# Reordering the first loads of a two-layer decoder trunk: one semaphore per input, adaLN columns in pairs, a held GpSimd queue, and the first norm's squares and root moved forward

## What is computed

```python
c_act = jax.nn.silu(c)
for l in range(DEPTH):                       # DEPTH = 2
    mod = c_act @ ada_w[l] + ada_b[l]        # 6 * 1024 columns
    shift1, scale1, gate1, shift2, scale2, gate2 = jnp.split(mod, 6)
    h = rms_norm(x, norm1_g[l]) * (1.0 + scale1) + shift1
    proj = h @ w_in[l]                       # q, k, v of two mixers, two gates
    ...                                      # sliding-window and stick-breaking attention
    x = x + gate1 * (merged @ w_out[l])
    h2 = rms_norm(x, norm2_g[l]) * (1.0 + scale2) + shift2
    x = x + gate2 * peer_ffn(h2, ...)        # top-16 of 128^2 experts, 8 heads, rows gathered
return rms_norm(x, final_g)
```

## Time and profile before

| | us |
|---|---|
| median of 3 runs | 1884.69 |
| lowest, highest | 1884.15, 1887.4 |
| the profiled execution's own time | 1883.45 |
| its span in the trace | 1881.6 |
| busy: TensorE / VectorE / ScalarE / GpSimd | 1534.5 / 1402.4 / 584.2 / 513.1 |

### The profile page before, as it was taken

How to read it: one execution, slowest core, us unless ns; L and a number is a source line. 1 busy time by engine, 2 the same in 40 slices (tenths; PEclk the granted TensorE clock), 3 DMA queues, 4 the chain that set the end, 5 groups by cost and what they waited for, 6 DMA issues and landing times.

```text
span 1881.6 us, 18314 instructions
## 1 busy us (share of the span) xinstructions
PE 1534.5 (82%) x6060; PEld 915.2 (49%) x6060; DVE 1402.4 (75%) x3392; ACT 584.2 (31%) x1322; POOL 513.1 (27%) x564
## 2 busy tenths in 40 slices
PE   1989899887787788787888999998778688777786
PEld 0978889333333333333367889963333233333332
DVE  5889899877767777765578989997777776767555
ACT  2445544322222122122244555522212212212221
POOL 0000003433333333333300000234333333333330
PEclk9999999988898989989999999999998999998989
DMA  8665778999999999999947668699999999999994
GB/s 349 227 222 187 257 247 365 418 421 422 421 421 421 421 421 421 422 421 421 421 179 239 192 214 285 265 414 421 421 422 421 421 421 421 422 421 421 422 422 194
DMA packets 104639, 675.73 MB, mean 359 GB/s; under 512 B 12000, under 2 KB 12128, under 8 KB 32352
## 3 DMA queue, kind: packets, MB, share of 16 engines
q0 software_dynamic: 80640, 587.24, 76.4%
q1 hardware_dynamic: 23904, 87.32, 13.3%
HBM read 673.46 MB, written 1.05 MB: 358 GB/s over the span
## 4 chain that ended last, share of the span: by engine, by line
DMA 45%; PE 32%; DVE 17%; ACT 2%; issue 2%; SPq 1%; DVEq 0%; ACTq 0%
DMA big<-pairs,big 22%; DMA late<-pairs,big 21%; PE yac L623 13%; PE acc L406 11%; DVE big L1079 2%; DVE big L925 2%; DVE wsp L385 2%; DVE late L1079 2%; DMA big<-ada_pairs 2%; PE pg L406 2%; PE acc L506 1%; PE yac L585 1%; SPq L432 1%; ACT big L777 1%; DMA big<-ada 1%
## 5 line engine op out<-in xcount | busy, mean ns | idle before, releaser
L623 PE MATMUL yac<-big 128*128 128x512 f32 x1184 | 565.3, 631 | 132.1 <-ACT big L777 132.1
L623 PE MATMUL yac<-late,big 128*128 128x512 f32 x864 | 433.9, 657 | 119.9 <-ACT big L777 119.9
L623 PEld LDWEIGHTS yac<-big 128*128 128x128 f32 x1184 | 232.7, 202 | 456.3 <-issue 269.1
L1265 POOL DMA_INDIRECT big<-pairs,big x296 | 284.6, 961 | 432.0 <-PE yac L623 391.4
L623 PEld LDWEIGHTS yac<-late,big 128*128 128x128 f32 x864 | 176.5, 210 | 374.3 <-issue 208.9
L1265 POOL DMA_INDIRECT late<-pairs,big x216 | 202.7, 938 | 380.7 <-PE yac L623 329.9
L406 PE MATMUL acc<-hs,wsp 128*128 128x256 f32 x2208 | 285.8, 288 | 0.0
L406 PEld LDWEIGHTS acc<-hs,wsp 128*128 128x128 f32 x2208 | 272.8, 194 | 7.3 <-issue 6.5
L1079 DVE CUSTOM_DVE_ANT_0 big<-big,acc 128x1024 f32<-128x1024 f32 x148 | 179.0, 1219 | 116.2 <-DMA big<-pairs,big 116.0
L768 ACT ACTIVATE big<-big 128x4 f32<-128x4 f32 (+1 forms) x138 | 28.3, 205 | 715.5 <-DVE big L1079 715.5
L777 ACT ACTIVATE big<-con,big 128x128 f32<-128x128 f32 x512 | 164.7, 390 | 247.4 <-DVE big L1094 247.2
(11 more groups left out here) (148 smaller groups left out, 1162.4 us busy)
## 6 DMA issues: line engine op xcount, KB each, us to landing
raw<-stream SPq DMA_DIRECT2D x140, 512.0 KB
big<-ada_pairs POOLq DMA_DIRECT2D x48, 1024.0 KB, 7.2
big<-ada SPq DMA_DIRECT2D x16, 512.0 KB, 15.3
big<-pairs,big POOLq DMA_INDIRECT x296, 21.5
late<-pairs,big POOLq DMA_INDIRECT x216, 22.3
big<-subkeys SPq DMA_DIRECT2D x2, 1024.0 KB, 13.2
x<-xT SPq DMA_DIRECT2D x1, 1024.0 KB, 7.1
outT<-big SPq DMA_DIRECT2D x1, 1024.0 KB, 3.9
```

Source lines behind the costliest of these rows:

```text
L623: mm = pe.matmul(yac[:, 2 * t + w, :], diag(n), row(n)[:, D + w * 512:D + (w + 1) * 512], start=(n % (SLOTS // TT) == 0), stop=(n % (SLOTS ...
L1265: g.indirect_dma_start(row(n), None, pairs, bass.IndirectOffsetOnAxis(ap=col(Q_IDX + n).bitcast(U32), axis=0)).then_inc(row_in[n % RING], 16)
```

## The change

- The five inputs are issued in another order and on four semaphores: `pos` and `con` on `con_in`, `cB` on `c_in`, `x` on `x_in`, `final_g` on `gain_in`. TensorE and VectorE wait for `con_in` at their start, ScalarE for `c_in`, and for `x_in` ahead of the squares; VectorE waits for `gain_in` ahead of the last norm.
- The 16 `ada` blocks are loaded and taken in pairs (k, 8 + k), each pair on a semaphore of its own. SP's order is: pos, con, cB, pairs 0 and 1, x, par, pairs 2 and 3, chunk 0, pairs 4 and 5, chunk 1, pairs 6 and 7, chunks 2 and 3, final_g, subkeys.
- GpSimd's first load of adaLN pairs in layer 0 waits until pair 7 has landed.
- ScalarE makes squares and root first, then the high parts of chunks 0 and 1, and that of chunk 2 behind `modulated`.
- VectorE no longer waits for the sine tables. It takes the reciprocal behind pair 4, the low part of chunk 0 behind pair 5, of chunk 1 behind pair 6, and of chunk 2 behind `source`. Behind pair 7 come a join and `next_mods`.

```diff
-            sp.dma_start(con[:, :], consts).then_inc(inputs_in, 16)
-            sp.dma_start(x[:, :], xT).then_inc(inputs_in, 16)
-            sp.dma_start(cact, cB).then_inc(inputs_in, 16)
-            sp.dma_start(cosT[:, :].bitcast(I32), pos).then_inc(inputs_in, 16)
-            sp.dma_start(fg[:, :], final_g).then_inc(inputs_in, 16)
+            sp.dma_start(cosT[:, :].bitcast(I32), pos).then_inc(con_in, 16)
+            sp.dma_start(con[:, :], consts).then_inc(con_in, 16)
+            sp.dma_start(cact, cB).then_inc(c_in, 16)
...
-            for a in range(N_ADA1):
-                sp.dma_start(ada_first(a), ada[a, :, :]).then_inc(first_ada_in[a // 4], 16)
-                if a % 4 == 3:
-                    sp.dma_start(raw[:, a // 4, :], stream[a // 4, :, :]).then_inc(landed[a // 4], 16)
+            def load_first(k):
+
+                for a in (k, KD + k):
+                    sp.dma_start(ada_first(a), ada[a, :, :]).then_inc(first_ada_in[k], 16)
+
+            load_first(0)
+            load_first(1)
+            sp.dma_start(x[:, :], xT).then_inc(x_in, 16)
+            sp.dma_start(par[:, :], params[0, :, :]).then_inc(params_in, 16)
+            load_first(2)
+            load_first(3)
+            load(0, 0, 0, 0)
+            load_first(4)
+            load_first(5)
+            load(1, 0, 0, 0)
+            load_first(6)
+            load_first(7)
+            load(2, 0, 0, 0)
+            load(3, 0, 0, 0)
+            sp.dma_start(fg[:, :], final_g).then_inc(gain_in, 16)
...
-            pe.wait_ge(inputs_in, 80)
+            pe.wait_ge(con_in, 32)
...
-            act.wait_ge(inputs_in, 80)
+            act.wait_ge(c_in, 16)
...
                 if L == 0:
-                    for m in range(AHEAD):
-                        act_high(act, L, m)
+                    act.wait_ge(x_in, 16)
                     squares(0, KD)
                 root(nth(L, 2, 1))
+                if L == 0:
+                    act_high(act, L, 0)
+                    act_high(act, L, 1)
                 act.wait_ge(mod_ready, nth(L, 1, 1))
                 modulated(L, 0)
+                if L == 0:
+                    act_high(act, L, 2)
...
+            def inverse(norm):
 
                 dve.wait_ge(rms_done, norm)
                 d.link(v.reciprocal(rms, rms))
+
+            def normalised(norm, gain, low=None):
+
+                if norm > 1:
+                    inverse(norm)
+                else:
+                    dve.wait_ge(mod_ready, 1)
...
-            dve.wait_ge(inputs_in, 80)
+            dve.wait_ge(con_in, 32)
...
-            dve.wait_ge(rope_table, 1)
...
-            for a in range(N_ADA1):
-                dve.wait_ge(first_ada_in[a // 4], 64)
-                d.mark(ada_column(ada_first(a), modn[:, a:a + 1]))
-            d.clear()
+            for k in range(KD):
+                dve.wait_ge(first_ada_in[k], 32)
+                for a in (k, KD + k):
+                    d.mark(ada_column(ada_first(a), modn[:, a:a + 1]))
+                if k == 4:
+                    inverse(1)
+                if k == 5:
+                    dve_low(dve, 0, 0)
+                if k == 6:
+                    dve_low(dve, 0, 1)
 
             for L in range(depth):
                 if L == 0:
-                    for m in range(AHEAD):
-                        dve_low(dve, L, m)
+                    d.join()
                     next_mods(L)
                 source(L, 0, 0)
+                if L == 0:
+                    dve_low(dve, L, 2)
                 d.clear()
...
+                if L == 0:
+
+                    pool.wait_ge(first_ada_in[KD - 1], 32)
                 for a in range(0, N_ADA, AP):
                     load_ada(a)
```

More of the change, by code:

```diff
@@ L218, in build @@
         yac = ctx.enter_context(nc.psum_tensor("yac", [P, 4, 512], F32))
-        inputs_in = sem("inputs_in")
+        con_in = sem("con_in")
+        c_in = sem("c_in")
+        x_in = sem("x_in")
+        gain_in = sem("gain_in")
         landed = [sem(f"landed{s}") for s in range(RAW)]
@@ L224, in build @@
         subkeys_in = sem("subkeys_in")
-        first_ada_in = [sem(f"first_ada_in{n}") for n in range(4)]
+        first_ada_in = [sem(f"first_ada_in{n}") for n in range(KD)]
         ada_in = [sem(f"ada_in{g}") for g in range(AB)]
@@ L438, in _ @@
                     sp.wait_ge(topk_done, L * UNITS)
-                sp.dma_start(par[:, :], params[L, :, :]).then_inc(
-                    params_in, 16)
+                    sp.dma_start(par[:, :], params[L, :, :]).then_inc(
+                        params_in, 16)
                 sp.dma_start(col(B_SUB, 2 * CH), subkeys[L, :, :]).then_inc(
@@ L891, in _ @@
             dve.sem_inc(pg_free, 2)
-            def normalised(norm, gain, low=None):
+            def inverse(norm):
                 dve.wait_ge(rms_done, norm)
                 d.link(v.reciprocal(rms, rms))
+            def normalised(norm, gain, low=None):
[3 more added lines that the diff above has]
+                    dve.wait_ge(mod_ready, 1)
                 for k in range(KD):
@@ L1236, in _ @@
                 d.clear()
+            dve.wait_ge(gain_in, 16)
             normalised(2 * depth + 1, fg)
```

## The result

The changed kernel takes 1872.47 us, median of 4 runs (1869.63 to 1873.13), against 1884.42 of the kernel before in the same sitting (1882.48 to 1887.4). The ratio is 0.9931, 95% interval 0.9912 to 0.9949. That is 12.0 us off, against 11.8 forecast. The profiled execution took 1873.13 us, its span is 1871.3.

What follows compares the result with a forecast made beforehand. Transfers bound the start, then VectorE's work behind the last one. 6.3 us from the last transfer plus 7.6 from behind it, less 2.0, gave about 11.8: 1884.69 - 11.8 = 1873 us, range 1867 to 1879.

Steps and rivals of the forecast that it cites:

- The ruler: Transfers at the start: 400 KB per us from 3.15 us, pair 4 at 22.9, the last column there 6.3 us sooner.
- VectorE's own time: Work from pair 4 at 22.9 us runs without a wait; first normalised piece at 36.7 instead of 48.49, 11.8 us sooner.
- The covers: Places claimed hidden: root 4.6 us early, chunk 2's low part in a 1.56 us gap, chunk 4 with 2.5 us margin.
- The clock: TensorE's first products: no change taken, 2.8 us either way; rival with a second place, 1868.4 (chance 0.08) or 1877.6 (0.09).
- The end: Everything behind the first product hangs on data and moves as a block, so the whole 11.8 us is kept.
- the slow 24 products that the prediction names: TensorE's 24 products taking 4.68 us against 2.88 in the long piece; slow stretch could go or double, 1.8 us either way.
- the sum: Whole kernel: profiled execution 1883.45 us less 11.8 is 1871.6; for the median, 1884.69 less 11.8 is 1873.
- one us for each us that the chunk lands: ScalarE's high part of chunk 4: price of one us for each us that it lands after 45.9.
- the slower rival: Chunk 4 comes too late for ScalarE's high part, holding up TensorE; landing at 65 us gives 1888 us, chance 0.02.
- The list of places where the clock can change the time: Two TensorE places: the first products, 2.8 us either way, and 24 later slow products, 1.8 us either way.
- the bound from the spread of runs: Whole kernel's time: the median against the highest run allows 2.7 us.

Runs made afterwards that it cites:

- hold_alone: Kernel before with only GpSimd's first loads held until the fourth group of columns has landed; 1877.76 us, ratio 0.9966.
- no_hold: Changed kernel without the wait ahead of GpSimd's first adaLN pairs; 1878.11 us, ratio 0.9968.
- work_alone: Kernel before with only the changed order of VectorE's and ScalarE's work, loads, groups and hold as before; 1879.25 us.
- one_sem: Changed kernel with all five inputs first in line and on one semaphore; 1871.84 us.
- fours: Changed kernel with VectorE waiting for two pairs (four columns) at a time; 1875.17 us.
- changed_again: The changed kernel run once more, unaltered; 1874.73 us, median of 7 runs, ratio 0.9946 to before.
- warm_long: Changed kernel plus unused TensorE products behind the landings of pairs 4 to 7 (4, 5, 4 and 10); 1871.0 us.
- work_behind: Changed kernel with three low parts and the reciprocal put back behind the last column; 1874.83 us.
- gap_fill_warm: Changed kernel with chunks 0 and 1 issued later, reciprocal behind pair 3, chunk 1's low part later, and 21 unused TensorE products; 1870.77 us.
- late_chunk: Changed kernel with 1536 KB of unused loads behind subkeys, in front of chunk 4; 1872.34 us.

## Why the prediction was right

**The ruler** held. It was 0.4 us early (pair 4 at 23.32 against 22.9). In the first 4 us the changed kernel moves about 130 KB less than the kernel before (8 and 271 GB/s against 28 and 315 in its two halves), which is 0.3 us of it. The number of queues is not the reason: hold_alone, one queue in the old order, has 303 GB/s at 2 to 4 us, and no_hold, two queues in the new order, 240. So it goes with the order of the first loads; why stays open. From there the distances hold, and the rate of one queue is that of two.

**VectorE's own time** held to a tenth: from pair 4 to the first normalised piece 13.75 us against 13.8. Its row has no wait behind pair 4, as forecast. The first product came 11.4 us sooner instead of 11.8, all of the difference being the ruler's start. (The ends of pairs 0 and 1, put at 12.2 and 14.5, do not follow from a start at 9.6 and 2.3 us a pair, which give 11.9 and 14.2; measured are 12.0 and 14.3, and nothing hangs on them.)

**The covers** held: the root at 20.63 us against 20.6 (between 20.6 and 22.3 in the kernels with this start, so the tenth is chance; the cover was enough each time), the third low part in the gap behind `source`, GpSimd's load at 32.56 against 32, chunk 4 taken at 45.28 with no wait for it. work_alone, one_sem, fours and the hold show each step with its size, all within 0.6 us of the expected place.

**The clock** was put at no change, with 2.8 us either way. It rose 3.7 us behind the first product instead of 5.9, which gave 1.0 us at the third chunk; changed_again has it later, 5.4 us behind, and the chunk at 46.82. So this 1.0 us is a matter of the execution and not of the change. The place was right as one where the clock can change the time, but with the full clock from the first product on, in warm_long, 1.5 us are won against the kernel before and not 2.8, since the pieces of the input then set the pace.

**The end.** I kept the whole gain, on the ground that all behind hangs on data. The table bears that out: in all kernels the gain at the first product is there at layer 1's first gather within 0.8 us. In the first profiled pair 12.4 us at the third chunk are 11.1 at the first gather and 10.3 at the end. In changed_again 11.5 are 11.4 and 12.3.

What is lost between the third chunk and the first gather goes with TensorE's clock. In every trace it falls to half at two places there, one within 80 to 110 us (the slow 24 products that the prediction names) and one within 245 to 275, which it does not name. The stretches of these two, in the kernel before, in the changed kernel and in fours (busy, count, clock, DMA, GB/s):

```profile
80.00:110.00 30.00, 24.42 (x169) 0.89 0.70 246
245.00:275.00 30.00, 25.49 (x184) 0.94 0.70 249
```

```profile
80.00:110.00 30.00, 23.09 (x154) 0.89 0.72 239
245.00:275.00 30.00, 25.52 (x182) 0.89 0.55 189
```

```profile
80.00:110.00 30.00, 23.08 (x144) 0.83 0.72 252
245.00:275.00 30.00, 25.67 (x185) 0.94 0.66 226
```

Before, the two places cost 5.1 us of full-speed time (0.11 and 0.06 of 30 us each), in the changed kernel 6.6, in fours 6.9. The 14 traces fall into the same two groups by the time from third chunk to first gather: the four with 0.89 and 0.94 (before, hold_alone, changed_again, one_sem) need 227.8 to 228.2 us, the nine that lose more at one of the places (the first in work_behind, fours and gap_fill_warm, the second in the other six) 228.7 to 229.6. The one exception is late_chunk, 229.3 us with 0.89 and 0.94, and it has its 1.2 us from the late chunk. One and the same kernel stands in both groups (the changed one and changed_again), so which it is belongs to the execution. No run sets the clock there on purpose: the cause rests on this grouping and on the size, 1.5 us of clock against 1.2 us of time between the two executions of the changed kernel. The 1.2 us that the first profiled pair loses from the second gather (11.5 us sooner) to the end are not traced.

Over the groups of runs the medians give 12.0 and 8.9 us, the forecast lying between. That the first is within 0.2 us of 11.8 is luck: the runs cannot tell so little, and the profiled pair, on which the sum stands, gives 10.3.

**What failed** is a price beside the sum: "one us for each us that the chunk lands" late. late_chunk puts it at 1.2 to 1.3 us for 2.8, as TensorE has two chunks in hand, and this stays at least until TensorE's products at 202 us. It would have made the slower rival even less likely. The list of places where the clock can change the time lacked the one at 250 us, which took 1.5 us more in the first profile than before. And the bound from the spread of runs, 2.7 us, holds for the two medians (2.3 apart) but not for single runs, which reach 3.8 us above the median in changed_again.

## What to carry to other kernels

Where a start is bound by transfers, count the bytes in front of each consumer and fit a line to two waits of the trace: it places every later arrival after a reordering. Then lay the consuming engine's work into the arrivals; the last wait without work in hand sets the end, and an earlier start before it is worth nothing. Transfers from another queue that nobody needs yet are in that count too, and holding them costs one wait.

## What the hardware showed beyond expectation

One queue alone moves what two move (414 against 419 GB/s). TensorE's clock, kept up by unused products, fell about 4.3 us after they had ended, just under the products that it was for; with unused products that ended 1.4 and 0.9 us before the real ones it stayed up. At the full clock 32 products that could take 3.8 us took 5.1, since half of them follow the pieces of their operand, one each 0.40 us. And the same kernel, twice profiled, differed by 1.2 us in one stretch of 228 by the length of a spell at half clock: a difference of that size between two single traces should be checked against the rows of the clock before it is credited to a change.
